# Last pair of the second FFN by tokens, and norm sums over squares added beforehand, in a hybrid encoder layer

## The chip, the cores and the metric

The kernel runs on one core of a Trainium2 chip. Its time is the device time of one launch in microseconds (us), the median of several runs; what a change is worth is judged against the same kernel's runs before it. Engines are named as in the profile: PE (TensorE, matmuls), PEld (its weight loads), DVE (VectorE), ACT (ScalarE), POOL (GpSimd), SP (the engine that issues most DMAs).

## The reference

1088 tokens (1024 of a prompt, 64 of a sample) of width 1024 pass one layer. All is float32.

```python
def _rmsnorm(x, g):
    xf = x.astype(jnp.float32)
    y = xf * lax.rsqrt(jnp.mean(xf * xf, axis=-1, keepdims=True) + EPS)
    return (y * g.astype(jnp.float32)).astype(x.dtype)

def _swiglu_half(x, g, w_gate, w_up, w_down):
    h = _rmsnorm(x, g)
    return 0.5 * ((jax.nn.silu(h @ w_gate) * (h @ w_up)) @ w_down)
...
        xp = xp + _swiglu_half(xp, g_ffn1[l], w1_gate[l], w1_up[l], w1_down[l])
        dp, kp, vp, Cp, n_p, mp = _mix_prompt(xp, rows, *mix_w)
        xp = xp + dp
        xp = xp + _swiglu_half(xp, g_ffn2[l], w2_gate[l], w2_up[l], w2_down[l])
        xp = _rmsnorm(xp, g_final[l])
```

The hidden width of an FFN is 2816. The mixer (projection, windowed attention, mLSTM, output projection) begins with its own `_rmsnorm`.

## The kernel before

**Layout.** The residual x stands transposed, features on partitions: `X` and `X2` are [128, 8, 1088], eight blocks of 128 features by 1088 tokens. Every float32 product that counts is made of three matmuls of the type fp32r (`three_pass`, L248 to L250): high part by high part, high by low, low by high. The high part of an operand is a copy in fp32r by ACT, the low part a subtraction by DVE or POOL.

**Tiles.** The mixer and the down projections work on three token tiles `NTILE` of 364, 362 and 362 tokens; the first stages of an FFN and the output projection on four tiles of 272 (`OT`).

**FFN down projection.** Hidden features go in 11 pairs of 128 (`PAIRS`, the last one is `LAST`). For each pair `pe_down` (L1165 on) makes, for each of three token tiles n and eight output blocks m, six matmuls into one of six banks (`DOWN_BANK`: 0, 1, 2, 3, 6, 7); `dve_x` (L1183 on) adds half of the bank to x. So one pair is 24 groups of six matmuls on PE and 24 additions on DVE (L1194). `AB` holds the pair's activations (high and low), `WB` its weights; `down_high` (ACT) and `down_low`/`down_a_low` (DVE/POOL) prepare them one pair ahead.

**End of the kernel.** After the last pair PE transposes x back to tokens (L2479): nine blocks b of 128 tokens (the last has 64), two halves of 512 features each, into the eight banks in turn. ACT squares and sums each half (L1850), DVE adds the two sums (L2185), ACT takes the root (L1852), DVE the reciprocal (L2187) and multiplies each half by it and by the gain `GF` into `YO` (L2193). SP sends the block out (L1401, L1403). POOL loads `GF` (L1600) after the last matmul of the last pair, because `GF` lies in the memory of that pair's weights `WBe`.

**Norm sums.** A norm in the transposed layout needs, per token, the sum of squares over 1024 features, on every partition. ACT squares x in two halves of four blocks (`norm_square` L264, `start_square` L737); PE multiplies each of the eight blocks of squares with a matrix of ones (`ONES`), in plain float32, into one bank (`norm_sum` L283, `start_sum` L743). Then ACT takes the root (L268, L751), DVE the reciprocal (L288, L755) and the scaled x (L296, L771), ACT the high part (L274, L782), DVE the low part (L303, L786). In the mixer's norm the three sums stand in PE's order inside the last pair of the first FFN: the sum of tile 0 after group m=4 of tile 1, that of tile 1 after group m=5 of tile 2, that of tile 2 after the first projection chain (c=0). The projection chains `M1` (L250 and neighbours, operands HH, HL, WGH, WGL) run tile by tile, four chains c to a tile at first; before chains 0, 4 and 8 PE waits (`norm_wait`) for both halves of the low part of that tile. After chain c, `head_sums(c-1)` (L2217) sums squares per head, and waits for the root of the head sum before it. In the norm of the second FFN the sums of tiles 0 to 2 stand after output chains 37, 41 and 45, that of tile 3 after the first gate chain.

**Order.** Each engine's program is written out by hand; engines meet at counting semaphores. An engine waits in its own order, so everything behind a waiting instruction waits too. `st.sq`, `st.ss`, `st.rs`, `st.rc` count squares, sums, roots and reciprocals; `s_.xadd` counts the additions to x, `fin.y` the halves of `YO` written, `x_tr` the transposed halves. In the mixer's norm ACT's order is: squares of tile 0, root 0, both squares of tile 1, high parts of tile 0, first squares of tile 2, root 1, second squares of tile 2; then, after it has read chain c=0, high parts of tile 1 and root 2; after c=2, high parts of tile 2.

## Time and profile before

| | |
|---|---|
| median of 3 runs | 2059.22 us (2057.47 to 2061.34) |
| the profiled execution's own time | 2060.87 us |
| its span | 2059.0 us |
| mean granted clock of PE | 0.993 |
| PE busy | 2022.5 us |
| DVE, POOL, ACT busy | 1165.6, 711.6, 691.8 us |
| FFN 1 / mixer begins / FFN 2 norm / last pair of FFN 2 | to about 777 us / 777 us / 1249 us / 2009 us |

The profile is of one execution; times inside it count from its span's start. A matmul's listed duration overlaps the next one's, so what a matmul costs PE is the distance between starts, not the duration. A plain float32 matmul with `ONES` leaves two records in the profile; the counts there (x16 for eight) follow from that.

### The profile page before, as it was taken

To read this page: it belongs to the slowest core of one execution; us is meant where nothing else is said; L and a number is where in the kernel's file an instruction comes from. 1 tells how busy PE (TensorE), PEld (TensorE's weight loads), DVE (VectorE), ACT (ScalarE), POOL (GpSimd) and SP (SyncE) were. 2 spreads that over 40 slices of the span, in tenths; PEclk is the share of its full clock that TensorE was granted. 3 is DMA by queue.
4 is the path that set the end of the run, shared out by engine and by line. 5 is a ranking of instruction groups with operands and counts; after the bars stand their busy time and mean duration, and the time that the engine had idled before them with its cause. 6 is when DMAs were issued, how large, how long until landed. Compare 5 with 4: busy or idle time off the path is not lost.

```text
span 2059.0 us, 38383 instructions
## 1 busy us (share of the span) xinstructions
PE 2022.5 (98%) x14285; PEld 1978.0 (96%) x14285; DVE 1165.6 (57%) x2016; ACT 691.8 (34%) x1371; POOL 711.6 (35%) x732
## 2 busy tenths in 40 slices
PE   7999999999999999999999999999999999999996
PEld 7999999999999999989998999999999999999996
DVE  6755444454666666754445654664454544666665
ACT  6333333333111133733335542433333333311112
POOL 2265655554211110131222430046555555411110
PEclk8999999999999999999999999999999999999999
DMA  8122221215422120342331733212112122632202
GB/s 256 43 84 74 87 68 62 88 68 210 156 91 84 42 74 4 99 121 88 99 101 59 209 85 107 74 64 95 62 62 94 62 94 84 235 102 102 91 0 98
DMA packets 151956, 194.62 MB, mean 95 GB/s; under 512 B 11448, under 2 KB 117464, under 8 KB 151872
## 3 DMA queue, kind: packets, MB, share of 16 engines
q1 hardware_dynamic: 144176, 173.85, 25.8%
q0 software_dynamic: 7696, 19.63, 3.0%
q8 instruction: 55, 0.90, 0.2%
q14 instruction: 29, 0.24, 0.0%
HBM read 142.43 MB, written 50.96 MB: 94 GB/s over the span
## 4 chain that ended last, share of the span: by engine, by line
PE 91%; issue 3%; DVE 2%; ACT 2%; DMA 1%; POOL 0%; SPq 0%; DVEq 0%; ACTq 0%; POOLq 0%
PE bank L248 28%; PE bank L250 28%; PE bank L249 28%; PE bank L2275 1%; PE bank L2294 1%; PE bank L2285 1%; PE bank L743 1%; PE bank L283 1%; DVE YO L2193 1%; DMA XIN<-in_x_prompt 1%; DVE RSC L1892 0%; PE bank L2383 0%; PE bank L2375 0%; PE bank L2385 0%; PE bank L2344 0%
## 5 line engine op out<-in xcount | busy, mean ns | idle before, releaser
L1194 DVE SCALAR_TENSOR_TENSOR X<-bank,X 128x362 f32<-128x362 f32 (+1 forms) x528 | 275.1, 533 | 191.0 <-PE bank L250 191.0
L248 PE MATMUL bank<-HH,WGH 128*128 128x362 f32 (+2 forms) x808 | 264.1, 327 | 0.0
L249 PE MATMUL bank<-HL,WGH 128*128 128x362 f32 (+2 forms) x808 | 255.2, 316 | 0.0
L250 PE MATMUL bank<-HH,WGL 128*128 128x362 f32 (+2 forms) x808 | 255.1, 316 | 0.0
L248 PE MATMUL bank<-FC,WR 128*128 128x272 f32 x768 | 223.3, 291 | 2.2 <-ACT X L693 2.0
L250 PE MATMUL bank<-FC,WR 128*128 128x272 f32 x768 | 222.7, 290 | 0.0
L249 PE MATMUL bank<-FC,WR 128*128 128x272 f32 x768 | 221.9, 289 | 0.0
L589 DVE TENSOR_TENSOR PV<-bank,PV 128x272 f32<-128x272 f32 x280 | 122.5, 439 | 148.0 <-PE bank L250 107.9
L656 POOL TENSOR_TENSOR SA<-SA,PV 128x272 f32<-128x272 f32 x160 | 136.5, 874 | 112.8 <-DVE PV L589 109.7
L248 PEld LDWEIGHTS bank<-HH,WGH 128*128 128x128 f32 x808 | 152.8, 189 | 14.7 <-issue 13.0
L469 DVE TENSOR_TENSOR WR<-RAWU,WR 128x512 fp32r<-128x512 f32 x100 | 86.4, 864 | 131.6 <-ACT WR L464 131.6
L248 PE MATMUL bank<-ABe,WBe 128*128 128x362 f32 (+1 forms) x480 | 158.0, 329 | 0.0
L248 PE MATMUL bank<-ABo,WBo 128*128 128x362 f32 (+1 forms) x480 | 157.6, 328 | 0.0
L250 PE MATMUL bank<-ABo,WBo 128*128 128x362 f32 (+1 forms) x480 | 157.1, 327 | 0.0
L250 PE MATMUL bank<-ABe,WBe 128*128 128x362 f32 (+1 forms) x480 | 157.0, 327 | 0.0
L249 PE MATMUL bank<-ABo,WBo 128*128 128x362 f32 (+1 forms) x480 | 157.0, 327 | 0.0
L249 PE MATMUL bank<-ABe,WBe 128*128 128x362 f32 (+1 forms) x480 | 156.9, 327 | 0.0
L249 PEld LDWEIGHTS bank<-HL,WGH 128*128 128x128 f32 x808 | 152.7, 189 | 1.6
L250 PEld LDWEIGHTS bank<-HH,WGL 128*128 128x128 f32 x808 | 152.6, 189 | 0.0
L248 PEld LDWEIGHTS bank<-FC,WR 128*128 128x128 f32 x768 | 145.2, 189 | 3.1 <-issue 2.2
L249 PEld LDWEIGHTS bank<-FC,WR 128*128 128x128 f32 x768 | 145.6, 190 | 0.0
L250 PEld LDWEIGHTS bank<-FC,WR 128*128 128x128 f32 x768 | 145.5, 189 | 0.0
(350 smaller groups left out, 5564.1 us busy)
## 6 DMA issues: line engine op xcount, KB each, us to landing
asp<-SA SPq DMA_DIRECT2D x44, 544.0 KB, 3.1
AR<-asp SPq DMA_DIRECT2D x22, 1088.0 KB, 5.0
RAWG<-in_w_gate SPq DMA_DIRECT2D x22, 1024.0 KB, 5.9
RAWU<-in_w_up SPq DMA_DIRECT2D x22, 1024.0 KB, 5.2
RAWDe<-in_w_down SPq DMA_DIRECT2D x12, 1024.0 KB, 4.9
RAW<-in_w_in SPq DMA_DIRECT2D x22, 512.0 KB, 3.6
RAWDo<-in_w_down SPq DMA_DIRECT2D x10, 1024.0 KB, 5.1
xsp<-X SPq DMA_DIRECT2D x8, 1088.0 KB, 6.1
```

Source lines behind the costliest of these rows:

```text
L248: nc.tensor.matmul(bank[:, 0:w], w_hi, rhs_hi, start=first, stop=False)
L249: nc.tensor.matmul(bank[:, 0:w], w_hi, rhs_lo, start=False, stop=False)
L250: return nc.tensor.matmul(bank[:, 0:w], w_lo, rhs_hi, start=False, stop=last)
L283: mm = nc.tensor.matmul(BANK[NORM_BANK[n]][:, 0:w], ONES[:, :], SQH[:, k, t0:t0 + w], start=(k == 0), stop=(k == KT - 1))
L469: nc.vector.tensor_tensor(WR[:, o, 1], weight(o, q0, mat), WR[:, o, 0].bitcast(F32), ALU.subtract).then_inc(s_.lo, 1)
L589: nc.vector.tensor_tensor(out, bank, add, ALU.add).then_inc(s_.ev, 1)
L656: nc.gpsimd.tensor_tensor(gated(j, slot), gated(j, slot), PV[j][:, tile], ALU.mult).then_inc(s_.mul, 1)
L743: mm = nc.tensor.matmul(BANK[4 + n][:, 0:HT], ONES[:, :], SQT[:, kh, k], start=(kh == 0 and k == 0), stop=(kh == 1 and k == 3))
L1194: nc.vector.scalar_tensor_tensor(out=x, in0=BANK[DOWN_BANK[i % 6]][:, 0:w], scalar=0.5, in1=x, op0=ALU.mult, op1=ALU.add).then_inc(s_.xadd, 1)
L2193: nc.vector.scalar_tensor_tensor(out=YO[0:L, b % 4, c], in0=BANK[(2 * b + half) % 8][0:L, :], scalar=f[:, 3:4], in1=GF[0:L, c], op0=ALU.mu ...
L2275: mm = nc.tensor.matmul(BANK[2 + i // 2][:, (i % 2) * 256:(i % 2) * 256 + 256], QB[rows, par, 2 * g_ + hl // 2, :], KW[rows, par, 0 if g_ ...
L2285: tr = nc.tensor.transpose(BANK[4 + w][:, i * P:(i + 1) * P], SP[:, i, w * P:(w + 1) * P], IDENT[:, :])
```

## The change

1. **The last pair of FFN 2 by tokens.** `pe_down` and `dve_x` of that pair and the transposes behind it are gone. In their place `pe_token_block` takes each block b of tokens and each half of 512 features: four transposes of x put x into the bank, by tokens, and six fp32r matmuls (activations stationary, 512 weight columns moving) add the pair's product on top, in the same bank. The half of the FFN's factor 0.5 goes into the weights' high and low parts. Banks are `TOKEN_BANK`: 4 and 5, 0 and 1, 2 and 3, 6 and 7.
2. **The end follows block by block.** ACT and DVE read the same bank as before, now each block as soon as PE has left it. `GF` lies in the memory of the first pair's weights, and POOL loads it after the second pair. The last block goes out in two DMAs of half its width.
3. **Norm sums.** POOL adds the four blocks of squares of a half to two and then to one (in place), and PE multiplies two blocks with `ONES` where it multiplied eight. Each sum now waits for POOL (`st.add`), not ACT.
4. **Places.** Sum of tile 1 in the mixer's norm: after group m=7 of tile 2 (was m=5). Sum of tile 2: after chain c=2 (was c=0). Sum of tile 3 in FFN 2's norm: after the second gate chain (was the first). Chains 0, 4 and 8 wait for the first half of the low part at their start and for the second at k=4.

```diff
-        GF = place("GF", [P, D], F32, rD)
+        GF = place("GF", [P, D], F32, rWG)
...
-            for k in range(KT):
-                if k % 4 == 0:
-                    pe.wait_ge(st.sq, 9 + 2 * n + k // 4 + 1)
-                mm = nc.tensor.matmul(BANK[NORM_BANK[n]][:, 0:w], ONES[:, :], SQH[:, k, t0:t0 + w], start=(k == 0), stop=(k == KT - 1))
+            for h in range(2):
+                pe.wait_ge(st.add, 4 * n + 2 * h + 2)
+                mm = nc.tensor.matmul(BANK[NORM_BANK[n]][:, 0:w], ONES[:, :], SQH[:, 4 * h, t0:t0 + w], start=(h == 0), stop=(h == 1))
             mm.then_inc(st.ss, 1)
+
+        def norm_add(pool, n, h):
+            t0, w = NTILE[n]
+            k = 4 * h
+            pool.wait_ge(st.sq, 9 + 2 * n + h + 1)
+            nc.gpsimd.tensor_tensor(SQH[:, k:k + 2, t0:t0 + w], SQH[:, k:k + 2, t0:t0 + w], SQH[:, k + 2:k + 4, t0:t0 + w], ALU.add).then_inc(st.add, 1)
+            pool.wait_ge(st.add, 4 * n + 2 * h + 1)
+            nc.gpsimd.tensor_tensor(SQH[:, k, t0:t0 + w], SQH[:, k, t0:t0 + w], SQH[:, k + 1, t0:t0 + w], ALU.add).then_inc(st.add, 1)
...
+        def start_add(pool, n, kh):
+            done = 12 + 4 * n + 2 * kh
+            pool.wait_ge(st.sq, 15 + 2 * n + kh + 1)
+            nc.gpsimd.tensor_tensor(SQT[:, kh, 0:2], SQT[:, kh, 0:2], SQT[:, kh, 2:4], ALU.add).then_inc(st.add, 1)
+            pool.wait_ge(st.add, done + 1)
+            nc.gpsimd.tensor_tensor(SQT[:, kh, 0], SQT[:, kh, 0], SQT[:, kh, 1], ALU.add).then_inc(st.add, 1)
...
-                start_chain(pe, f, 0, 0, 0)
-                start_sum(pe, 3)
-                for i in range(1, 4):
+                for i in range(4):
                     start_chain(pe, f, 0, 0, i)
+                    if i == 1:
+                        start_sum(pe, 3)
...
+        TOKEN_BANK = (4, 0, 2, 6)
...
+        def pe_token_block(pe, b):
+
+            L, t0 = (P if b < NB else DEC), b * P
+            done = 264 + LAST * 24
+            if b == 0:
+                pe.wait_ge(s_.alo, LAST * 2 + (22 + 2))
+                pe.wait_ge(s_.dlo, LAST * 2 + (22 + 2))
+            if b < 4:
+                pe.wait_ge(s_.xadd, done - 24 + (8, 20, 22, 24)[b])
+            else:
+                pe.wait_ge(fin.y, 2 * (b - 3))
+            for half in range(2):
+                bank, c = token_bank(b, half), slice(512 * half, 512 * half + 512)
+                for k in range(4):
+                    nc.tensor.matmul(bank[0:L, k * P:(k + 1) * P], X[:, 4 * half + k, t0:t0 + L], IDENT[:, :], is_transpose=True, start=k == 0, stop=False)
+                for d in range(2):
+                    a_hi, a_lo = (AB[2][:, i, d, t0:t0 + L] for i in range(2))
+                    w_hi, w_lo = (WB[2][:, i, d, c] for i in range(2))
+                    nc.tensor.matmul(bank[0:L, :], a_hi, w_hi, start=False, stop=False)
+                    nc.tensor.matmul(bank[0:L, :], a_hi, w_lo, start=False, stop=False)
+                    mm = nc.tensor.matmul(bank[0:L, :], a_lo, w_hi, start=False, stop=d == 1)
+                mm.then_inc(x_tr, 1)
...
-            pool.wait_ge(s_.dmm, 2 * 264)
+            pool.wait_ge(s_.dmm, 264 + 48)
...
-            pe_down(pe, 0, LAST, 0, 2, between=lambda: norm_sum(pe, norm, 1), at=5)
+            pe_down(pe, 0, LAST, 0, 2, between=lambda: norm_sum(pe, norm, 1), at=KT - 1)
```

Where the instructions stand. First PE's order at the second mixer sum, before; ABe and WBe are the last pair's operands.

```order
1889 L250 MATMUL bank3<-ABe_83,WBe_86 128x362
1890 L283 MATMUL bank5<-SQH_96,ONES_144 128x362 x8
1891 L248 MATMUL bank6<-ABe_83,WBe_86 128x362
1892 L249 MATMUL bank6<-ABe_83,WBe_86 128x362
1893 L250 MATMUL bank6<-ABe_83,WBe_86 128x362
```

And the same sum on PE in the changed kernel (HH, HL, WGH and WGL are the first projection chain's operands).

```order
1901 L250 MATMUL bank7<-ABe_83,WBe_86 128x362
1902 L282 MATMUL bank5<-SQH_96,ONES_144 128x362 x2
1903 L248 MATMUL bank0<-HH_51,WGH_54 128x364
1904 L249 MATMUL bank0<-HL_52,WGH_54 128x364
1905 L250 MATMUL bank0<-HH_51,WGL_55 128x364
```

The sum has two matmuls for eight and has moved behind the last two groups of the last pair, to the mixer's first chain.

POOL's order between the first FFN and the mixer's first store, before.

```order
134 L1159 TENSOR_TENSOR ABe_83<-AR00_88,ABe_83 128x1088 x2
135 L1455 DMA out_7<-in_cache_k 16x512
136 L1456 DMA out_8<-in_cache_v 16x512
137 L1458 MEMSET RAW4_58 128x1024
138 L1476 DMA zqk<-ZST_97 128x364
```

And in the changed kernel (its last four rows stand once more, for the third tile, ahead of the store).

```order
137 L1504 MEMSET RAW4_58 128x1024
138 L289 TENSOR_TENSOR SQH_96<-SQH_96 128x2x364
139 L291 TENSOR_TENSOR SQH_96<-SQH_96 128x364
140 L289 TENSOR_TENSOR SQH_96<-SQH_96 128x2x364
141 L291 TENSOR_TENSOR SQH_96<-SQH_96 128x364
142 L289 TENSOR_TENSOR SQH_96<-SQH_96 128x2x362
143 L291 TENSOR_TENSOR SQH_96<-SQH_96 128x362
144 L289 TENSOR_TENSOR SQH_96<-SQH_96 128x2x362
145 L291 TENSOR_TENSOR SQH_96<-SQH_96 128x362
```

Twelve additions have come between the memset and the store, four for each tile. Eight pairs of the form 128x544 and 128x272 stand likewise ahead of POOL's first weight sum of FFN 2.

Last, PE's order at the end of the kernel, before.

```order
6188 L248 MATMUL bank7<-ABe_83,WBe_86 128x362
6189 L249 MATMUL bank7<-ABe_83,WBe_86 128x362
6190 L250 MATMUL bank7<-ABe_83,WBe_86 128x362
6191 L2479 MATMUL bank0<-IDENT_143,X_49 128x128 x4
6192 L2479 MATMUL bank1<-IDENT_143,X_49 128x128 x4
```

And the first half of the first token block in the changed kernel.

```order
6047 L1197 MATMUL bank4<-IDENT_143,X_49 128x128 x4
6048 L1201 MATMUL bank4<-WBe_86,ABe_83 128x512
6049 L1202 MATMUL bank4<-WBe_86,ABe_83 128x512
6050 L1203 MATMUL bank4<-WBe_86,ABe_83 128x512
6051 L1201 MATMUL bank4<-WBe_86,ABe_83 128x512
6052 L1202 MATMUL bank4<-WBe_86,ABe_83 128x512
6053 L1203 MATMUL bank4<-WBe_86,ABe_83 128x512
6054 L1197 MATMUL bank5<-IDENT_143,X_49 128x128 x4
```

The transposes no longer stand behind all matmuls of the pair; four of them open each of 18 groups, followed by six matmuls of 512 columns.

## Rows read from the trace of the kernel before

**Rows 1.** The page: PE's busy time and the chain that ended last.
```profile
PE 2022.5 (98%) x14285; PEld 1978.0 (96%) x14285; DVE 1165.6 (57%) x2016; ACT 691.8 (34%) x1371; POOL 711.6 (35%) x732
PE 91%; issue 3%; DVE 2%; ACT 2%; DMA 1%; POOL 0%; SPq 0%; DVEq 0%; ACTq 0%; POOLq 0%
```
**Rows 2.** Timeline (start, duration, engine, line, operation), PE, first mixer sum.
```profile
755.95 5.05 PE L283 MATMUL bank<-SQH,ONES 128*128 128x364 f32 x16
...
761.01 0.32 PE L249 MATMUL bank<-ABe,WBe 128*128 128x362 f32 x1
```
**Rows 3.** Timeline, PE, first sum of FFN 2's norm.
```profile
1254.16 3.83 PE L743 MATMUL bank<-SQT,ONES 128*128 128x272 f32 x16
...
1257.95 0.29 PE L249 MATMUL bank<-HL,WGH 128*128 128x272 f32 x1
```
**Rows 4.** POOL: one line's view (min/median/max ns), and one group by form (mean).
```profile
L656 POOL TENSOR_TENSOR SA<-SA,PV x160: 762/773/1678, 110.7 to 1773.7; 128x272 f32<-128x272 f32 x160
...
L1159 POOL TENSOR_TENSOR ABe<-AR,ABe 128x1088 fp32r<-128x1088 f32 x20 | 50.4, 2543 | 176.6 <-ACT ABe L1144 176.6
```
**Rows 5.** Timeline, ACT and DVE, the mixer's norm: squares to low parts.
```profile
751.79 1.42 ACT L264 ACTIVATE SQH<-X 128x1456 f32<-128x1456 f32 x1 [2.58 <-DVE X L1194]
753.69 1.22 DVE L1267 TENSOR_TENSOR WGL<-RAW,WGH 128x1024 fp32r<-128x1024 f32 x1
761.64 2.43 DVE L288 RECIPROCAL SQH<-SQH 128x364 f32<-128x364 f32 x1 [4.28 <-ACT SQH L268]
771.10 1.66 DVE L303 TENSOR_TENSOR HL<-SQa,HH 128x1456 fp32r<-128x1456 f32 x1
773.56 1.66 DVE L303 TENSOR_TENSOR HL<-SQb,HH 128x1456 fp32r<-128x1456 f32 x1
795.56 1.41 ACT L274 ACTIVATE HH<-SQb 128x1448 fp32r<-128x1448 f32 x1
798.92 0.57 ACT L1632 ACTIVATE RSC<-bank,EPSC 128x364 f32<-128x364 f32 x1
```
**Rows 6.** Timeline, POOL and DVE side by side in FFN 2.
```profile
1509.96 1.30 POOL L452 TENSOR_TENSOR RAWG<-RAWG,SS 128x512 f32<-128x512 f32 x1 [1.72 <-DVE WR L469]
1510.33 1.47 DVE L469 TENSOR_TENSOR WR<-SS,WR 128x512 fp32r<-128x512 f32 x1
```
**Rows 7.** Timeline, ACT, last squares of FFN 2's norm.
```profile
1296.03 2.10 ACT L737 ACTIVATE SQT<-X 128x1088 f32<-128x1088 f32 x2
```
**Rows 8.** Timeline, PE: last pair's first and last matmul, and transposes.
```profile
2009.08 0.33 PE L248 MATMUL bank<-ABe,WBe 128*128 128x364 f32 x1
2032.67 0.32 PE L250 MATMUL bank<-ABe,WBe 128*128 128x362 f32 x1
2033.62 3.71 PE L2479 MATMUL bank<-IDENT,X 128*128 128x128 f32 x32 [0.63 <-DVE X L1194]
```
**Rows 9.** Timeline, PE: 16 transposes between two fp32r chains, FFN 1.
```profile
26.79 1.91 PE L687 MATMUL bank<-IDENT,XIN 128*128 128x128 f32 x16
...
28.67 0.29 PE L249 MATMUL bank<-FC,WR 128*128 128x272 f32 x1
```
**Rows 10.** Timeline, DVE, ACT and SP: the end, first block, then last block.
```profile
2035.60 1.28 ACT L1852 ACT_TABLE_LOAD   x1
2037.28 0.16 DVE L2185 TENSOR_TENSOR FS<-FS 128x1 f32<-128x1 f32 x1 [3.71 <-DMA GF<-in_g_final]
2039.33 0.15 DVE L2185 TENSOR_TENSOR FS<-FS 128x1 f32<-128x1 f32 x1
...
2052.49 0.58 ACT L1850 ACTIVATE JUNK<-bank 64x512 f32<-64x512 f32 x1
2053.57 0.14 DVE L2185 TENSOR_TENSOR FS<-FS 64x1 f32<-64x1 f32 x1
2055.69 0.55 SPq L1403 DMA_DIRECT2D out<-YO  x1
```
**Rows 11.** Windows: stretch, length, busy of PE, PEld, DVE, ACT, POOL; clock, DMA, GB/s.
```profile
26.00:30.00 4.00, 4.00 (x36) 4.00 (x35) 4.00 (x10) 2.08 (x3) 0.00 (x0) 1.00 1.03 400
2040.00:2050.00 10.00, 6.31 (x38) 4.55 (x35) 8.03 (x19) 7.07 (x26) 0.00 (x0) 0.83 0.66 264
```

More of the change, by code:

```diff
@@ L740, in start_sum @@
             for kh in range(2):
-                pe.wait_ge(st.sq, 15 + 2 * n + kh + 1)
-                for k in range(4):
-                    mm = nc.tensor.matmul(BANK[4 + n][:, 0:HT], ONES[:, :], SQT[:, kh, k], start=(kh == 0 and k == 0), stop=(kh == 1 and k == 3))
+                pe.wait_ge(st.add, 12 + 4 * n + 2 * kh + 2)
+                mm = nc.tensor.matmul(BANK[4 + n][:, 0:HT], ONES[:, :], SQT[:, kh, 0], start=(kh == 0), stop=(kh == 1))
             mm.then_inc(st.ss, 1)
+        def start_add(pool, n, kh):
[4 more added lines that the diff above has]
+            nc.gpsimd.tensor_tensor(SQT[:, kh, 0], SQT[:, kh, 0], SQT[:, kh, 1], ALU.add).then_inc(st.add, 1)
         def scale_row(f, n):
@@ L1126, in up_pe, with by_token @@
                     pe_stage(pe, f, p, i // 2, i % 2)
+        def by_token(f, p):
+            return f == 1 and isinstance(p, int) and p == LAST
         def a_raw(f, odd, start):
@@ L1146, in down_high @@
                 act.wait_ge(s_.d_in1 if odd else s_.d_in0, loads)
-                nc.scalar.activation(WB[which][:, 0, i], RAWD[odd][:, i], ACT.Copy).then_inc(s_.dhi, 1)
+                nc.scalar.activation(WB[which][:, 0, i], RAWD[odd][:, i], ACT.Copy, scale=0.5 if by_token(f, p) else 1.0).then_inc(s_.dhi, 1)
         def down_low(dve, f, p, odd, i, start=False):
@@ L1271, in loads_until, with unit_chain @@
             return (j - 4) // 4 + 1 if j % 4 == 0 else (j - j % 4) // 4 + 1 + (j % 4 == 1)
-        def unit_chain(pe, n, slot, bank, tiles=NTILE, k0=0, k1=KT):
+        def unit_chain(pe, n, slot, bank, tiles=NTILE, k0=0, k1=KT, second=None):
             t0, w = tiles[n]
             for k in range(k0, k1):
+                if k == 4 and second is not None:
+                    pe.wait_ge(second, n + 1)
                 mm = three_pass(bank, w, WGH[:, slot, k], WGL[:, slot, k], HH[:, k, t0:t0 + w], HL[:, k, t0:t0 + w], k == k0, k == k1 - 1)
@@ L1395, in _ @@
             ffn_sp(sp, 1, a["w2_gate"][0], a["w2_up"][0], a["w2_down"][0])
[L1398 removed]
+            for b in range(NB):
                 sp.wait_ge(fin.y, 2 * b + 2)
[L1400 to L1403 removed]
+                sp.dma_start(o[0][0, b * P:(b + 1) * P, :], YO[:, b % 4, :]).then_inc(fin_out[b % 4], 16)
+            for half in range(2):
+                c = slice(512 * half, 512 * half + 512)
+                sp.wait_ge(fin.y, 2 * NB + half + 1)
+                sp.dma_start(o[1][0, :, c], YO[0:DEC, NB % 4, c]).then_inc(fin_out[NB % 4], 16)
             for i in range(4):
[L1405 removed]
+                sp.wait_ge(fin_out[i], 16 * ((NB - i) // 4 + 1 + (i == NB % 4)))
         @block.gpsimd
@@ L1458, in _ @@
             nc.gpsimd.memset(RAW4[:, 1, :, :], 0.0).then_inc(z.padded, 1)
+            for n in range(3):
+                for h in range(2):
+                    norm_add(pool, n, h)
             flat = lambda ap: ap.rearrange("p h d -> p (h d)")
@@ L1593, in _ @@
             pool.dma_start(o[10][0, 0].rearrange("h d -> d h"), CNS[:, :, LD]).then_inc(m_.cout, 16)
+            for n in range(4):
+                for kh in range(2):
+                    start_add(pool, n, kh)
             pool.wait_ge(m_.cout, 96)
@@ L2175, in _ @@
             down_dve(dve, 1)
-            for n in range(3):
-                dve_x(dve, 1, LAST, n)
             dve.wait_ge(const_in, 16 * 12)
@@ L2242, in _ @@
             for c, (j, n) in enumerate(M1):
-                if c < 12 and c % 4 == 0:
-                    norm_wait(pe, norm, n)
+                opens = c < 12 and c % 4 == 0
+                if opens:
+                    pe.wait_ge(norm.lo0, n + 1)
                 pe.wait_ge(z.lo, j)
@@ L2252, in _ @@
                     pe.wait_ge(z.zg, NORMED.index(c - 4) + 1)
-                unit_chain(pe, n, j % 4, BANK[c % 4])
+                unit_chain(pe, n, j % 4, BANK[c % 4], second=norm.lo1 if opens else None)
                 if c == C1 - 1:
@@ L2257, in _ @@
                     head_sums(c - 1)
-                if c == 0:
+                if c == 2:
                     norm_sum(pe, norm, 2)
@@ L2467, in _ @@
             down_pe(pe, 1)
-            for n in range(3):
-                pe_down(pe, 1, LAST, 0, n)
-            pe.wait_ge(s_.xadd, 2 * 264)
             for b in range(NB + 1):
-                L = P if b < NB else DEC
-                if b >= 4:
-                    pe.wait_ge(fin.y, 2 * (b - 3))
-                for half in range(2):
-                    for k in range(4):
-                        tr = nc.tensor.transpose(BANK[(2 * b + half) % 8][0:L, k * P:(k + 1) * P], X[:, 4 * half + k, b * P:b * P + L], IDENT[:, :])
-                    tr.then_inc(x_tr, 1)
+                pe_token_block(pe, b)
 _INS = ["x_prompt", "x_sample", "cache_k", "cache_v", "state_C", "state_n", "state_m", "g_ffn1", "w1_gate", "w1_up", "w1_down",
```

23 lines of the change are left out of this document (10 added, 13 removed).

## The prediction

> **What bounds the kernel now.** I read the page first: PE is busy for 98% of the span, and 91% of the chain that ended last is PE's [rows 1]. So an instruction taken from PE shortens the kernel by what it costs there, unless PE then waits for what is late next. I read the two norms in the timeline next, since the sums stand in PE's order: PE has no idle time around them, and the squares are ready when it comes [rows 2, 3, 5]. Last I read the end. PE's last fp32r matmul starts at 2032.67 [rows 8], the span ends at 2059.0: 26 us in which PE only transposes and the rest waits, first for `GF`, to 2037.28, then nine times for one round of DVE and ACT, 2.05 us each (2037.28 to 2039.33), then for the last DMA, from 2055.69 to the span's end [rows 10]. This stretch is bound by DVE with ACT.
>
> **Sums off PE.** Eight matmuls with `ONES` at 364 columns take from 755.95 to 761.01, less one normal distance of 0.165 us: 4.9 us, 0.61 each [rows 2]. Six fewer: 3.65 us; three sums: 10.9 us. (The distance 0.165 is (2032.67 - 2009.08) / 143, the 144 matmuls of the last pair [rows 8].) In FFN 2's norm eight at 272 columns take 1254.16 to 1257.95, less about 0.13: 3.66 us, 0.455 each [rows 3]. Six fewer, four sums: 10.9 us. Together 21.8 us if nobody else becomes late.
>
> **What POOL's additions cost.** 272 elements take POOL 0.773 us, 1088 take 2.54 [rows 4], so by a line 364 take 0.97, 544 take 1.36 and 728 take 1.76. A half of squares costs POOL 2.7 us in the mixer, 2.1 us in FFN 2. POOL is otherwise idle at both places. But POOL and a DVE instruction that reads two operands from SBUF do not run side by side: DVE's L469, 128x512, takes 1.47 us where POOL's addition is under way at its start (1509.96 to 1511.26), and it ends some 0.5 us after that [rows 6]. The scale (L296), the low parts (L303) and the weights' low parts (L1267) are such instructions. The Trainium skill's GPSIMD Engine Reference, section Key points, says that the two engines share their SBUF interfaces and collide when a DVE instruction has two SBUF inputs; the trace agrees. Were additions and DVE's work free to run side by side, against that rule, the sum below would be about 3 us larger.
>
> **The mixer's norm, worked through.** (a) Tile 0. The second squares end at 753.21 [rows 5]; POOL would be done 2.7 us later, at 756.0. DVE's L1267 (1.22 us, wanted at 753.69 [rows 5]) falls in between and I give it to DVE first: 757.2. PE wants the sum at 755.95. Stall 1.3 us. Everything behind the sum on PE, the last pair's last eleven groups, waits with it. (b) Chain 0. The root now comes 2.0 us earlier than before (sum over at 758.6, not 760.57), and so does DVE's chain behind it: reciprocal (2.43), scale, low parts, which ended at 772.76 and 775.22 [rows 5]. But POOL's additions for tiles 1 and 2 fall into this chain's scale and second low part and take back a microsecond or more each. Low parts ready at about 771.5 and 775. PE, with two sums shorter (7.3 us) and 1.3 us late, comes to chain 0 at 770.5. It waits about 1.3 us at the start and 1.5 at k=4: 2.9 us. (c) The third sum has moved behind c=2, at about 785. ACT's root 2 stands ahead of its high parts of tile 2, and these ahead of its reads of chain 3. Root at 787, reciprocal and two scales on DVE (2.4 and 2 times 2.1) to 793.7, second high part to 795.2, then squares, copy and root for `head_sums` to 796.7; PE comes to the second `head_sums`, behind c=4, at 795.1. Stall 1.6 us. Before, this chain had slack: the high part started at 795.56 and the root at 798.92 with PE at 802 [rows 5]. Chains 4 and 8 find their low parts ready (783 and 796 at the latest). Sum for the mixer: 10.9 - 1.3 - 2.9 - 1.6 = 5.1. Bounds: 8 where DVE loses nothing to POOL, 2.5 where each meeting costs a full addition (1.8 us).
>
> **FFN 2's norm.** The squares of tiles 0 and 1 come several us before PE does. Those of tile 2 end about 1277.7 once PE is 5.4 us earlier; POOL, sharing with two low parts on DVE, is done at 1281.2, PE comes at 1280.5: 0.7 us. Those of tile 3 ended at 1298.13 [rows 7], now at 1290.6 because PE's output chains pace them; POOL needs two times 2.1 us and meets DVE's scale and low parts: 1294.2 to 1296. PE comes, behind its second gate chain, at 1294.5. I take 1.0 us. Sum: 10.9 - 1.7 = 9.2; bounds 10.5 and 6. POOL's weight sums for the next pair are in the same queue behind these additions, but wait for a transfer that comes later (they began at 1304.0 in the trace of before), so that costs nothing.
>
> **The last pair and the end.** Removed from PE: the 144 matmuls, 2009.08 to 2032.83, and 72 transposes. Added: 72 transposes and 108 matmuls of 512 columns. 32 transposes take 3.41 to 3.5 us [rows 8]: 0.107 each. A change from fp32r to transposes and back costs little: 16 transposes and the return take 28.67 - 26.79 - 0.13 = 1.75 us, of which 1.71 is the transposes [rows 9]; I take 0.05 for each of two in a block. No 512-column fp32r matmul is in the trace. The nearest is 0.165 us at 362 to 364 columns: in proportion 512 take 0.233; with only the 149 added columns at the full clock of 2.4 GHz, 0.165 + 0.062 = 0.227. I take 0.230. A block: 8 x 0.107 + 12 x 0.230 + 0.1 = 3.72 us, nine: 33.4 us. The last block has 64 tokens, but its moving columns are the same. PE starts at 2009.08 as before (block 0 needs the operands and eight additions of the pair before, which are long past; banks 4 and 5 are free) and ends at 2042.5, drained by 2042.7. ACT and DVE need 2.05 us for a block, under 3.72, so they keep up; block b+4 waits for a `YO` that was written about 10 us before. `GF`'s 3.7 us wait and the 1.28 us table load [rows 10] go beside PE's work. Behind the last matmul: squares 0.67, then from DVE's addition to SP's issue 2055.69 - 2053.57 = 2.12, then the DMA to the span's end 3.3 (2059.0 - 2055.69) [rows 10]; it now carries half, I give it the full 3.3. End at 2042.7 + 0.67 + 0.05 + 2.12 + 3.3 = 2048.8. Gain 10.2 us. Bounds: 13 (0.22 a matmul, 2.5 for the DMA) and 6 (0.24 a matmul and 0.15 a change). The low part of the last weights becomes a scalar_tensor_tensor; it runs some 15 us before it is needed and costs nothing.
>
> **Sum.** 5.1 + 9.2 + 10.2 = 24.5 us. The profiled span 2059.0 becomes 2034.5, its own time 2060.87 becomes 2036.4. That execution lies 1.65 above the median 2059.22, so the median becomes 2034.7; I say 2035.
>
> **Rivals.** (1) *No losses to POOL:* PE finds every sum ready and no chain late: 21.8 + 10.2 = 32.0, 2027. For: PE is the bound everywhere. Against: the arithmetic of (a), where POOL cannot be done in time. (2) *The sums give nothing:* DVE's norm chains become the bound and hand back all of what PE saves; only the end gains: 2049. For: chain 0 starts right behind the low parts already. Against: of FFN 2's norm only the last two sums meet a late partner. (3) *The clock falls in the token blocks:* in 2040 to 2050, where PE ran only transposes with gaps, its granted clock was 0.83 [rows 11]. If it went to 1.2 GHz, half, for all nine blocks, they would take 66.8 us instead of 33.4, and the kernel 2035 + 33.4 = 2068: slower. It turns slower from 24.5 / 3.72, between six and seven blocks at the half clock. Against: 26 to 30 us has transposes among fp32r chains at a clock of 1.00 [rows 11], and a block is three quarters fp32r. (4) *The matmuls on top of transposed x are slower:* at 0.46 us each instead of 0.23 they cost 24.8 us more, and the change is worth nothing. Nothing in the trace speaks for it.
>
> **How the numbers follow.** The forecast, with stalls anywhere within the bounds: 0.70, from 2059.2 - 31.5 = 2028 to 2059.2 - 14.5 = 2045. Rival 1: 0.12. Rival 2: 0.10. Rival 3: 0.04. Rival 4 and what I have not seen: 0.04. All bounds at once at their bad end are unlikely, so the range stops at 2043 and takes in rival 1's edge: 2026 to 2043. About 4 us, 0.2%, is what a measurement can tell from no change. Faster: 0.93; same: 0.03; slower: 0.04.
>
> **What would show it.** In the timeline of after: two-matmul sums of 1.2 and 0.9 us; a PE wait of some 1 us on POOL at the first mixer sum, 2 to 3 us at chain 0 for DVE's low parts, 1 to 2 us at the second `head_sums` on ACT, and one of about 1 us on POOL at the last sum of FFN 2's norm. At the end: token blocks 3.7 us apart, clock 1.00, and 6 to 6.5 us from PE's last matmul to the span's end. The prediction is wrong if the blocks lie over 4.2 us apart, if PE waits for `fin.y`, or if the waits at the norms sum to under 3 or over 15 us.

## The result, and the profile after

The changed kernel takes 2033.19 us (median of 4 runs, 2031.86 to 2033.58), the kernel before beside it 2059.31 (4 runs, 2057.47 to 2061.34). The ratio is 0.9872, 95% interval 0.9855 to 0.9889: 26 us faster. The forecast was 2035 in a range of 2026 to 2043. The profiled execution's own time is 2033.58, its span 2032.0.

The page of after first, PE's busy time and the chain that ended last, which answer to [rows 1]:

```profile
PE 1999.2 (98%) x14165; PEld 1954.1 (96%) x14165; DVE 1165.3 (57%) x1992; ACT 692.9 (34%) x1371; POOL 751.2 (37%) x760
PE 94%; DVE 2%; ACT 1%; DMA 1%; POOL 1%; issue 1%; SPq 0%; DVEq 0%; ACTq 0%; POOLq 0%
```

PE has 23 us less to do and is still the bound; POOL has 40 us more, nearly all of it additions of squares. DVE's total is the same although its last 24 additions to x are gone (12.7 us by the sum of their line): instructions that now meet POOL have grown by about as much, 32 scales of the second FFN's norm alone from 13.9 to 20.6 us. Then PE's waits in after, one group by line, releaser, total, times and longest:

```profile
PE bank L2265 <- ACT RSC L1684: 5.3, 4, 1.6
PE bank L248 <- DVE HL L310: 2.9, 2, 1.5
...
PE bank L744 <- POOL SQT L752: 0.9, 1, 0.9
```

The second and third groups are new, and the first had three waits before where it has four now. The timeline of PE in after shows where they stand in the mixer's norm (the last bracket is the idle time ahead of the instruction, and who ended it):

```profile
754.04 0.77 PE L282 MATMUL bank<-SQH,ONES 128*128 128x364 f32 x2
755.09 0.88 PE L282 MATMUL bank<-SQH,ONES 128*128 128x364 f32 x2 [0.28 <-POOL SQH L291]
...
769.62 0.43 PE L248 MATMUL bank<-HH,WGH 128*128 128x364 f32 x1 [1.49 <-DVE HL L310]
773.27 0.43 PE L248 MATMUL bank<-HH,WGH 128*128 128x364 f32 x1 [1.39 <-DVE HL L310]
...
794.85 0.85 PE L2265 MATMUL bank<-SQC,BD 128*128 128x364 f32 x2 [1.54 <-ACT RSC L1684]
```

The first sum (it answers to [rows 2]) loses 0.28 us to POOL, chain 0 loses 1.49 at its start and 1.39 at k=4 to DVE's low parts, the second `head_sums` 1.54 to ACT. In the second FFN's norm the same view has three sums that matter (they answer to [rows 3]):

```profile
1247.68 1.08 PE L744 MATMUL bank<-SQT,ONES 128*128 128x272 f32 x4
...
1275.14 0.72 PE L744 MATMUL bank<-SQT,ONES 128*128 128x272 f32 x2 [0.86 <-POOL SQT L752]
...
1287.81 1.45 PE L744 MATMUL bank<-SQT,ONES 128*128 128x272 f32 x4
```

The third sum waits 0.86 us for POOL. The fourth shows no wait, but its records span 1.45 us where the first sum's span 1.08: up to 0.4 us went there.

The end, PE in after: the transposes that open a half, in blocks 7 and 8, and the last matmul.

```profile
2018.96 0.60 PE L1197 MATMUL bank<-IDENT,X 128*128 128x128 f32 x4
2020.80 0.60 PE L1197 MATMUL bank<-IDENT,X 128*128 128x128 f32 x4
2022.64 0.60 PE L1197 MATMUL bank<-IDENT,X 128*64 128x128 f32 x4
...
2026.04 0.40 PE L1203 MATMUL bank<-WBe,ABe 128*64 128x512 f32 x1
```

Blocks lie 2022.64 - 2018.96 = 3.68 us apart. The windows of after over this stretch (length, busy time and count of PE, PEld, DVE, ACT, POOL, then the granted clock, DMA share and GB/s; they answer to [rows 11]):

```profile
1992.00:2010.00 18.00, 18.00 (x101) 15.16 (x101) 7.04 (x18) 7.86 (x21) 0.00 (x0) 1.00 0.22 89
2010.00:2026.00 16.00, 16.00 (x89) 12.75 (x88) 7.95 (x18) 7.37 (x22) 0.00 (x0) 1.00 0.33 132
```

PE has no gap and its clock is full, 2.4 GHz. Behind PE, the timeline of DVE, ACT and SP (they answer to [rows 10]):

```profile
1997.88 1.28 ACT L1904 ACT_TABLE_LOAD   x1
...
2027.19 0.15 DVE L2233 TENSOR_TENSOR FS<-FS 64x1 f32<-64x1 f32 x1 [1.50 <-ACT JUNK L1902]
...
2027.89 1.40 DVE L2241 SCALAR_TENSOR_TENSOR YO<-bank,FS,GF 64x512 f32<-64x512 f32 x2
2028.67 1.19 SPq L1449 DMA_DIRECT2D out<-YO  x2
```

The table load lies beside PE's first blocks. From PE's last matmul (2026.04 + 0.40) to the span's end are 5.56 us.

**Where the 27.0 us of the spans came from.** Six events stand in every kernel's trace, so distances between them can be subtracted: A, ACT's first squares of the mixer's norm; B, PE's second `head_sums`; C, PE's first sum of the second FFN's norm; D, PE's first matmul behind it that reads `FXb`, an operand of the gate and up chains; E, the start of the last pair; F, the span's end, which is given to 0.1 us only.

| kernel | start to A | A to B | B to C | C to D | D to E | E to F |
|---|---|---|---|---|---|---|
| before | 747.79 | 54.00 | 452.37 | 96.15 | 658.77 | 49.92 |
| after | 745.87 | 48.98 | 452.83 | 86.85 | 658.78 | 38.69 |
| gain | 1.92 | 5.02 | -0.46 | 9.30 | 0.0 | 11.23 |

A to B is the mixer's norm, C to D the second FFN's, E to F the end. Nothing is changed ahead of A. From B to C only the split wait of chain 8 is, and from D to E only the load of `GF` and the making of the last weights; PE waits for none of them. Kernels with the same instructions there differ by as much or more (start to A 745.19 to 747.82 in the table of all kernels, B to C 452.83 to 457.28 in three profiles of the changed kernel alone), so these differences are not counted as the change's.

### The profile page after: what moved, and what is told of

Its sections match the earlier page's. It is cut to its first block, busy times and chain, and to the rows that moved or that the text cites. A ratio compares the mean times of both kernels' runs of the same rounds, so it can differ in the third digit from the quotient of the medians.

```text
span 2032.0 us, 38145 instructions
## 1 busy us (share of the span) xinstructions
PE 1999.2 (98%) x14165; PEld 1954.1 (96%) x14165; DVE 1165.3 (57%) x1992; ACT 692.9 (34%) x1371; POOL 751.2 (37%) x760
## 4 chain that ended last, share of the span: by engine, by line
PE 94%; DVE 2%; ACT 1%; DMA 1%; POOL 1%; issue 1%; SPq 0%; DVEq 0%; ACTq 0%; POOLq 0%
PE bank L248 29%; PE bank L250 29%; PE bank L249 29%; PE bank L2324 1%; PE bank L2343 1%; PE bank L2334 1%; DMA XIN<-in_x_prompt 1%; PE bank L2265 0%; PE bank L2432 0%; PE bank L1203 0%; PE bank L1201 0%; PE bank L1202 0%; PE bank L2424 0%; PE bank L1197 0%; PE bank L2434 0%
## 5 line engine op out<-in xcount | busy, mean ns | idle before, releaser
L1237 DVE SCALAR_TENSOR_TENSOR X<-bank,X 128x362 f32<-128x362 f32 (+1 forms) x504 | 262.4, 533 | 178.9 <-PE bank L250 178.9
L517 ACT ACTIVATE SA<-SA 128x272 f32<-128x272 f32 x160 | 67.0, 429 | 227.7 <-DVE SA L591 118.6
L248 PE MATMUL bank<-ABe,WBe 128*128 128x362 f32 (+1 forms) x432 | 142.0, 329 | 0.0
L250 PE MATMUL bank<-ABe,WBe 128*128 128x362 f32 (+1 forms) x432 | 141.7, 328 | 0.0
```

What stands on the lines that cost most here:

```text
L248: nc.tensor.matmul(bank[:, 0:w], w_hi, rhs_hi, start=first, stop=False)
L250: return nc.tensor.matmul(bank[:, 0:w], w_lo, rhs_hi, start=False, stop=last)
L517: nc.scalar.activation(tile, tile, ACT.Silu).then_inc(s_.silu, 1)
L1237: nc.vector.scalar_tensor_tensor(out=x, in0=BANK[DOWN_BANK[i % 6]][:, 0:w], scalar=0.5, in1=x, op0=ALU.mult, op1=ALU.add).then_inc(s_.xadd, 1)
```

## The experiments

All are measured against the kernel before, in runs beside it. Some kernels are built from the changed kernel by undoing parts.

**1. The changed kernel again**, without an edit, as a partner for the parts.

> The changed kernel once more, as the measure for the three parts beside it. All theories: 2033 us or 26 us under the kernel before, within 2 us.

Measured: 2037.66 us beside 2062.02, ratio 0.9878 [0.9861, 0.9894]. A to B is 48.96, C to D 86.85, E to F 38.68: all three within 0.02 us of the first profile. B to C is 457.28, over 4 us more than in the other two profiles of this kernel (452.83 and 453.23). Part of that is the clock. In this trace the granted clock (seventh figure) is 0.50 to 0.65 from 1206 to 1214 us, where the first profile has 1.00 at the same place:

```profile
1208.00:1210.00 2.00, 2.00 (x9) 1.86 (x9) 1.75 (x7) 0.00 (x0) 0.00 (x0) 0.50 0.00 0
```

Two-microsecond windows like this one put its cost at 3.4 us at most: that is what the clock was short of full in them. So the stages that the change touches repeat closely (A to B and E to F to hundredths; C to D is 86.64 in a third profile), and the medians scatter at least in part by what happens elsewhere.

**2. The last pair by tokens alone.** Cut, against the changed kernel:

```diff
             for h in range(2):
-                pe.wait_ge(st.add, 4 * n + 2 * h + 2)
-                mm = nc.tensor.matmul(..., SQH[:, 4 * h, t0:t0 + w], ...)
+            for k in range(KT):
+                if k % 4 == 0:
+                    pe.wait_ge(st.sq, 9 + 2 * n + k // 4 + 1)
+                mm = nc.tensor.matmul(..., SQH[:, k, t0:t0 + w], ...)
...
-            for n in range(3):
-                for h in range(2):
-                    norm_add(pool, n, h)
```

> The last pair by tokens alone, all norm sums as before. My account (the end is worth 11.2 us by the two traces, 10.2 by the prediction's sum): 10 to 11.5 us under the kernel before, 2048 to 2049.5 us. Rival (the end's gain was helped by the sums, or the sums are worth all 22 us and the end little): under 7 us.

Measured: 2050.63, ratio 0.9941 [0.9927, 0.9954], 11.4 us under before. E to F is 38.75, 11.17 less than before; A to B 54.01 and C to D 96.15, as before.

**3. The mixer's sums alone**, and **4. the second FFN's sums alone.** In each the other norm and the end stand as before; in the third, for instance:

```diff
-            return f == 1 and isinstance(p, int) and p == LAST
+            return False
...
-            for n in range(4):
-                for kh in range(2):
-                    start_add(pool, n, kh)
```

> Only the three sums of the mixer's norm, with POOL's additions and the new places; FFN 2's norm and the end as before. My account: PE saves 10.9 us and waits 5 to 6 us more, net 4.5 to 5.5 us under the kernel before; in the trace, waits of 0.3 to 1.3 us for POOL at the first sum, 2.9 at chain 0, 1.5 at the second head sum. Rival (no losses to POOL and DVE): 10.9 us under. Rival (DVE's chain gives everything back): 0 to 1 us.

> Only the four sums of FFN 2's norm, with POOL's additions and the new place of the last; mixer's norm and the end as before. My account: 9 to 10 us under the kernel before, PE waiting about 1.3 us for POOL in all. Rival (POOL meets DVE at every sum): under 7 us.

Measured: the mixer's alone 2055.93, ratio 0.9964 [0.9951, 0.9978], 6.1 us under before; the second FFN's alone 2050.31, ratio 0.9943 [0.9928, 0.9957], 11.7 under. By stages: A to B 48.97 in the one (5.03 less) and 54.01 in the other; C to D 96.38 and 86.87 (9.28 less). By medians the three parts add up to 29.2, more than the whole gives beside them (24.4). By stages they add up to 11.17 + 5.03 + 9.28 = 25.5, and the whole is 11.23 + 5.02 + 9.30 = 25.6. So the parts are independent. The last two medians give 1 to 2.5 us more than their stages; the stretches that no part touches vary by more than that, so the surplus is put down to them, which is not shown.

**5. The three sums back at their old places**, with POOL's additions kept.

```diff
-                    if i == 1:
+                    if i == 0:
                         start_sum(pe, 3)
...
-            pe_down(pe, 0, LAST, 0, 2, between=lambda: norm_sum(pe, norm, 1), at=KT - 1)
+            pe_down(pe, 0, LAST, 0, 2, between=lambda: norm_sum(pe, norm, 1), at=5)
...
-                if c == 2:
+                if c == 0:
                     norm_sum(pe, norm, 2)
```

> The changed kernel with the three moved sums back at their old places (mixer's tile 1 after m=5, tile 2 after chain 0, FFN 2's tile 3 after the first gate chain), all additions still on POOL. Theory that the moves are what covers POOL's time: PE waits for POOL about 1.5 us more at the mixer's third sum and 3 to 3.5 us at FFN 2's last, the wait at the second head sum goes, net 3 to 5 us slower than the changed kernel. Rival (places do not matter, POOL is early enough): within 1 us of it, with POOL waits as before.

Measured: 2041.71 beside 2060.78, ratio 0.9903 [0.9886, 0.992]. PE's timeline of this kernel has three waits for POOL that the changed kernel doesn't have:

```profile
780.35 0.88 PE L282 MATMUL bank<-SQH,ONES 128*128 128x362 f32 x2 [2.45 <-POOL SQH L291]
...
1288.20 0.72 PE L744 MATMUL bank<-SQT,ONES 128*128 128x272 f32 x2 [1.13 <-POOL SQT L752]
1290.61 1.28 PE L744 MATMUL bank<-SQT,ONES 128*128 128x272 f32 x2 [1.68 <-POOL SQT L752]
```

A to B is 49.98 and C to D 91.34, 1.0 us more in the mixer and 4.5 more in the second FFN, 5.5 together, where 3 to 5 were expected. But not all of the 4.5 is waiting. Behind the last of these waits the granted clock was at half:

```profile
1290.00:1292.00 2.00, 1.39 (x4) 1.16 (x5) 2.00 (x3) 0.08 (x1) 0.55 (x1) 0.64 0.91 312
1292.00:1294.00 2.00, 2.00 (x11) 2.00 (x11) 2.00 (x3) 1.97 (x3) 1.56 (x1) 0.51 0.02 3
```

The matmuls of 272 columns stand 0.23 us apart there instead of 0.125, and from the sum's last matmul (1290.61) to the eleventh start behind it (1293.95) PE needs 3.3 us for what takes 1.8 in the changed kernel. So about 1.5 us of the 4.5 is the clock and 3.0 the waits with their restarts: the places are worth some 4 us by themselves, as expected. Whether the fall belongs to this kernel or to this one execution isn't known. In the mixer the wait for POOL (2.45) is partly paid for by the wait at the second `head_sums`, which is gone.

**6. ACT's high parts later.** The wait at the second `head_sums` was put down to ACT's order: its high parts of tile 2 stand ahead of its reads of chain 3. The timeline of ACT in the changed kernel:

```profile
790.00 1.43 ACT L274 ACTIVATE HH<-SQa 128x1448 fp32r<-128x1448 f32 x1 [3.46 <-DVE SQa L303]
792.02 1.42 ACT L274 ACTIVATE HH<-SQb 128x1448 fp32r<-128x1448 f32 x1 [0.60 <-DVE SQb L303]
793.34 0.45 ACT L1699 ACTIVATE SQC<-bank 128x364 f32<-128x364 f32 x1
793.69 0.56 ACT L1702 ACTIVATE ZST<-bank,GQ 128x364 f32<-128x364 f32 x1
794.14 0.57 ACT L1684 ACTIVATE RSC<-bank,EPSC 128x364 f32<-128x364 f32 x1
```

```diff
-                if c == 2:
+                if c == 3:
```

> The changed kernel; ACT makes the high parts of tile 2 after its reads of chain 3, not after those of chain 2. Theory (the new head-sum wait comes from ACT's order: high parts queued ahead of chain 3's squares and the root): the first of the four waits L2265 for RSC, 1.5 us, is gone, 1.5 us faster. Rival (the wait is that of a late DVE or of PE's own earlier arrival): it stays or moves to chain 8.

Measured: 2033.13, ratio 0.9865 [0.9849, 0.9882], 27.7 under before. PE's waits in this kernel, the same group as above:

```profile
PE bank L2265 <- ACT RSC L1684: 3.7, 3, 1.6
```

The fourth wait is gone, and A to B falls from 48.98 to 47.29: 1.69 us, the wait and its restart. The cause is shown.

**7. POOL's additions for tile 2 behind the low part.** The wait at k=4 was put down to POOL and DVE not running side by side. The timelines of DVE and POOL in the changed kernel:

```profile
760.22 3.96 DVE L303 SCALAR_TENSOR_TENSOR SQa<-X,GC,SQH 128x364 f32<-128x364 f32 x4
...
764.99 2.11 DVE L303 SCALAR_TENSOR_TENSOR SQb<-X,GC,SQH 128x364 f32<-128x364 f32 x4
...
767.91 1.66 DVE L310 TENSOR_TENSOR HL<-SQa,HH 128x1456 fp32r<-128x1456 f32 x1
...
770.37 2.85 DVE L310 TENSOR_TENSOR HL<-SQb,HH 128x1456 fp32r<-128x1456 f32 x1
```

```profile
759.79 0.97 POOL L291 TENSOR_TENSOR SQH<-SQH 128x362 f32<-128x362 f32 x1
761.83 1.96 POOL L289 TENSOR_TENSOR SQH<-SQH 128x724 f32<-128x724 f32 x1 [1.07 <-ACT SQH L264]
...
769.93 1.76 POOL L289 TENSOR_TENSOR SQH<-SQH 128x724 f32<-128x724 f32 x1 [4.92 <-ACT SQH L264]
771.77 2.28 POOL L291 TENSOR_TENSOR SQH<-SQH 128x362 f32<-128x362 f32 x1
```

A scale of the same form takes 2.11 us alone and 3.96 beside POOL, the same low part 1.66 and 2.85; POOL's short addition takes 0.97 alone and 2.28 beside DVE. The starts tell who pays. The second low part starts at 770.37, while POOL's long addition runs until 769.93 + 1.76 = 771.69, and it is that addition's remaining 1.3 us by which the low part is late, 1.2 us; the addition itself keeps its 1.76. POOL's short addition then starts at 771.77, while the low part runs until 773.22, and it is the short one that is stretched, by 1.3 us. So whoever starts second waits for the other to finish. The edit:

```diff
                 for h in range(2):
+                    if n == 2 and h == 0:
+                        pool.wait_ge(norm.lo1, 1)
                     norm_add(pool, n, h)
```

> The changed kernel; POOL's additions for the mixer's tile 2 start only when DVE has written the second low part of tile 0. Theory (POOL's addition and DVE's subtraction with two SBUF operands exclude each other): that low part takes 1.66 us again, not 2.85, and PE's wait at k=4 of chain 0 falls from 1.4 to 0.2 us; 1.2 us faster. Rival (the low part is late for another reason, and POOL merely slows itself): wait unchanged.

Measured: 2033.33, ratio 0.9869 [0.9853, 0.9886]. DVE's second low part in this kernel's timeline:

```profile
770.54 1.66 DVE L310 TENSOR_TENSOR HL<-SQb,HH 128x1456 fp32r<-128x1456 f32 x1
```

With POOL held back it takes 1.66 us, and PE's wait at k=4 is 0.20 instead of 1.39. A to B is 47.94, 1.04 less: the wait at the second `head_sums` has grown from 1.54 to 1.69. The collision is shown as the cause of the wait at k=4. It moved in part here too: the first scale of tile 1 takes 3.99 us in this kernel instead of 3.53, but PE doesn't come to wait for that tile's low parts.

**8. Both edits, and a third:** POOL's second additions for tile 1 wait for DVE's first scale, to free that scale too.

```diff
+                    if n == 1 and h == 1:
+                        pool.wait_ge(st.ht, 8 + 1)
```

> The two edits before together, and POOL's second additions for tile 1 wait for DVE's first scale of tile 0 (which took 3.96 us, 2.11 alone). Theory: the waits at chain 0 fall from 2.9 to about 1.0 us, the first head-sum wait is gone, in all 3 to 3.5 us faster than the changed kernel, 29 to 30 us under the kernel before. Rival (DVE's chain is paced by PE's additions to x and not by POOL): under 2 us.

Measured: 2033.55, ratio 0.9864 [0.9848, 0.9881]. Half of it came. The first scale fell from 3.96 to 2.46 us, but POOL's addition now met the second scale, which grew from 2.11 to 3.67: the collision had moved. And something else stood in chain 0, in the windows of this kernel:

```profile
770.00:772.00 2.00, 1.02 (x5) 1.03 (x6) 2.00 (x4) 1.65 (x2) 0.00 (x0) 0.94 0.00 0
772.00:774.00 2.00, 2.00 (x8) 2.00 (x8) 2.00 (x3) 0.00 (x0) 0.53 (x1) 0.50 0.00 0
774.00:776.00 2.00, 2.00 (x11) 2.00 (x10) 2.00 (x2) 1.41 (x1) 1.92 (x2) 0.70 0.00 0
```

and in PE's timeline:

```profile
770.98 0.43 PE L248 MATMUL bank<-HH,WGH 128*128 128x364 f32 x1 [1.84 <-DVE HL L310]
...
772.32 0.50 PE L248 MATMUL bank<-HH,WGH 128*128 128x364 f32 x1
772.62 0.51 PE L249 MATMUL bank<-HL,WGH 128*128 128x364 f32 x1
```

The granted clock (seventh figure) was 0.50, that is 1.2 GHz, in 772 to 774, a microsecond behind a wait of 1.84 us, and ten matmuls stand 0.30 us apart instead of 0.165. A to B is 47.22, hardly less than the 47.29 of experiment 6.

**9. The same kernel once more**, to see whether that fall belongs to it.

> The kernel with all three edits once more. In its first profile PE waited 1.84 us for the low part at the start of chain 0, and some 1 us later the granted clock was 0.50 in 772 to 774 us: ten matmuls of chain 0 stood 0.30 us apart instead of 0.165. Theory (what PE does around that wait brings the fall): the fall comes again at the same place, with ten or eleven matmuls 0.30 apart, and from ACT's first squares to PE's second head sum there are 47.2 us again. Rival (a chance event of that execution): no matmul of chain 0 is over 0.2 us from the next except at its start, and the stretch takes 46.1 us or less, as in the kernel with two edits (46.07).

Measured (2 runs): 2031.9 beside 2064.23, ratio 0.9846 [0.9817, 0.9874]. The rival held in substance. The same stretch in the windows of this run, and chain 0 in its timeline of PE:

```profile
770.00:772.00 2.00, 1.80 (x11) 1.50 (x10) 2.00 (x3) 0.00 (x0) 0.51 (x1) 1.00 0.00 0
772.00:774.00 2.00, 2.00 (x14) 2.00 (x13) 2.00 (x2) 1.57 (x2) 1.92 (x2) 1.00 0.00 0
```

```profile
769.00 0.43 PE L248 MATMUL bank<-HH,WGH 128*128 128x364 f32 x1 [1.68 <-DVE HL L310]
```

The wait was 1.68 here, the clock stayed full, and A to B is 46.15 (46.1 or less was said), 1.07 less than in experiment 8; at k=4 PE waited 0.20. So the fall comes in some executions and not in others, and costs about 1.1 us where it comes. What decides it stays open.

**10. The changed kernel as partner, and the two edits that had worked** (late high parts, POOL's wait for tile 2), without the third.

> The changed kernel itself, unchanged, as the partner of the two kernels beside it: 26 us under before, within 2; PE waits 1.5 us for ACT's root at the second head sum and 2.9 us for DVE's low parts at chain 0.

> Two edits to the changed kernel: ACT's high parts of tile 2 stand behind its reads of chain 3, and POOL's additions for tile 2 wait for the second low part of tile 0. Theory (a wait taken from PE's path comes off the time): PE's wait at the second head sum (1.5 us) and the one at k=4 of chain 0 (1.4 us) go, and nothing else becomes late: 2.7 us less than the changed kernel beside it, by medians 1 to 4.5 less. Rival (the time of the mixer's first chains is set elsewhere, by DVE or a DMA that comes later, so that waits only change their place): the same time within 1 us, with new PE waits of 2 to 3 us behind chain 4.

Measured beside before at 2061.28: the changed kernel 2037.48 (2034.7 to 2042.99), ratio 0.9892 [0.9875, 0.9909]; with the two edits 2034.29 (2032.05 to 2035.44), ratio 0.9869 [0.9852, 0.9887]. PE's timeline with the two edits:

```profile
770.23 0.44 PE L248 MATMUL bank<-HH,WGH 128*128 128x364 f32 x1 [1.48 <-DVE HL L310]
772.70 0.43 PE L248 MATMUL bank<-HH,WGH 128*128 128x364 f32 x1 [0.20 <-DVE HL L310]
...
792.57 0.78 PE L2267 MATMUL bank<-SQC,BD 128*128 128x364 f32 x2
```

A to B is 46.07 against 48.96: 2.89 us, where 2.7 was expected; the two single edits gave 1.69 and 1.04, 2.73 together. The medians differ by 3.2 and agree, but their intervals overlap; the stage distance carries the verdict that the two edits help. This is the version to keep: the third edit adds nothing to it (46.15 without the fall).

**11. The last block in one DMA** of full width instead of two of half of it.

```diff
-            for half in range(2):
-                c = slice(512 * half, 512 * half + 512)
-                sp.wait_ge(fin.y, 2 * NB + half + 1)
-                sp.dma_start(o[1][0, :, c], YO[0:DEC, NB % 4, c])...
+            sp.wait_ge(fin.y, 2 * NB + 2)
+            sp.dma_start(o[1][0, :, :], YO[0:DEC, NB % 4, :])...
```

> The changed kernel with the last block of 64 tokens written by one DMA of full width, behind both halves, instead of two of half the width. Theory (the last DMA is paid from its issue to the end, and the second half's issue was bound by DVE's last multiplication in either form): SP's issue comes at the same time as that of the second half before, about 20.6 us... that is 3.2 us before the end, and the landing takes 0.3 to 0.9 us longer for 256 KB than for 128: from PE's last matmul to the end 5.9 to 6.5 us, was 5.6. Rival (each of the two issues costs SP 0.6 us in a row, which is on the path): the single DMA ends 0.2 to 0.5 us earlier. By the medians neither can be seen; by the trace, from the last matmul to the span's end.

(The "20.6 us" in that text is a slip; what was meant follows it.) Measured: 2037.74, ratio 0.9887 [0.9869, 0.9906]. PE's last matmul in this trace, and SP's issue:

```profile
2030.40 0.40 PE L1203 MATMUL bank<-WBe,ABe 128*64 128x512 f32 x1
```

```profile
2033.68 0.55 SPq L1447 DMA_DIRECT2D out<-YO  x1
```

The span ends at 2037.0: 6.20 us behind PE's last matmul, was 5.56; E to F is 39.33, was 38.69. Splitting the last DMA is worth 0.64 us, and the rival (two issues in a row cost more than they bring) falls.

**The stages of all kernels**, in us:

| kernel | start to A | A to B | B to C | C to D | D to E | E to F |
|---|---|---|---|---|---|---|
| changed, 3 profiles | 745.87 to 746.44 | 48.96 to 48.98 | 452.83 to 457.28 | 86.64 to 86.85 | 658.78 to 661.18 | 38.68 to 38.69 |
| last pair alone | 746.63 | 54.01 | 453.40 | 96.15 | 660.16 | 38.75 |
| mixer alone | 747.78 | 48.97 | 452.97 | 96.38 | 658.61 | 49.79 |
| second FFN alone | 745.21 | 54.01 | 451.59 | 86.87 | 659.20 | 49.92 |
| old places | 747.64 | 49.98 | 452.21 | 91.34 | 660.28 | 38.75 |
| high parts later | 747.82 | 47.29 | 452.53 | 86.85 | 660.35 | 38.66 |
| POOL waits | 746.05 | 47.94 | 452.39 | 86.85 | 660.06 | 38.71 |
| two edits | 746.50 | 46.07 | 453.12 | 86.64 | 660.62 | 38.75 |
| three edits (first run) | 747.17 | 47.22 | 452.23 | 86.84 | 660.41 | 38.73 |
| three edits (second run) | 745.19 | 46.15 | 453.93 | 86.86 | 660.08 | 38.69 |
| last DMA whole | 746.70 | 48.97 | 454.32 | 86.86 | 660.82 | 39.33 |

## Why the prediction was right

**The whole.** 24.5 us were forecast from three terms; the same three stages give 5.02 + 9.30 + 11.23 = 25.55 in the traces. What is left to the 27.0 of the spans, 1.92 - 0.46, stands in stretches that hold the same instructions. It made the gain look a little larger in the first measurement; by medians it was 26.1 us there and 24.4 and 23.8 when the same kernel was run again.

**The mixer's norm: 5.1 forecast, 5.02 measured.** Its terms:
- The first sum, for POOL: 1.3 forecast, 0.28 seen. This step failed in two places. POOL ended at 753.21 + 1.82 = 755.03, that is 9.16 us behind A; the forecast had 757.2, 9.4 behind. And the forecast let PE stand from the start of the sum, while only the second of its two matmuls needs POOL's last addition: the first, 0.61 us, runs meanwhile.
- Chain 0: 2.9 forecast, 1.49 + 1.39 measured. Right, and the low parts came when the forecast said, 23.7 and 27.4 us behind A for 23.7 and 27.2. Experiment 7 shows the mechanism for the wait at k=4: POOL beside DVE. For the wait at the start it stays argued: it was 1.47 to 1.84 in every kernel with these sums, and experiment 8 only moved POOL from the first scale to the second.
- The second `head_sums`: 1.6 forecast, 1.54 measured; experiment 6 shows the mechanism, ACT's order.
- The waits sum to 4.7, and 10.9 - 4.7 is 6.2, not 5.0. The missing term is what a stop costs PE beside the wait, which the forecast put at nothing. The distances between starts give it: at k=4 the two matmuls stand 1.71 us apart, 1.55 over the normal distance for a wait of 1.39, and the next one follows after 0.27 instead of 0.165. Read so, the first sum costs 0.55, chain 0 1.75 and 1.65, and the second `head_sums` 1.70. A fifth stop has no wait in its row; a weight load waited there for DVE's addition to x, which stands behind the stretched first scale:

```profile
764.68 0.43 PE L248 MATMUL bank<-ABe,WBe 128*128 128x362 f32 x1
```

It starts 0.30 us behind the one before and costs 0.25 with its restart. Together that is 5.9, and 10.9 - 5.9 = 5.0. So two errors of the forecast, 1.0 us too much at the first sum and 1.2 us left out, cancelled: that the sum is closer than its parts is luck.

**The second FFN's norm: 9.2 forecast, 9.30 measured.** The third sum's wait was 0.86 (0.7 forecast), the fourth's at most 0.4 (1.0 forecast). The fourth term was too large for the same reason as in the mixer: the first matmul of the sum covers half a microsecond of the wait (POOL was done at 1288.47, PE had come at 1287.81). With their restarts the two sums cost 1.1 and 0.4 us, 1.5 together for the 1.7 forecast; another 0.2 us of the stage isn't accounted for. And POOL's weight sums behind the additions cost nothing, as said.

**The end: 10.2 forecast, 11.23 measured.** The blocks are right: 3.68 us for 3.72, no wait for `fin.y`, clock 1.00, the table load and `GF` hidden. PE's share of the end, 1993.31 to 2026.44, is 33.1 for 33.6: half of the 1.0 us. The other half lies behind PE, 5.56 us where the forecast had 6.1 and said 6 to 6.5. There the mis-sized term is the last DMA: 3.3 us were given to it because the whole one had taken that; split in two it takes 2.7 from the second issue (SP's two issues end at 2028.67 + 1.19, one takes 0.55, so the second began at 2029.31, and the span ends at 2032.0), and experiment 11 measures the split at 0.64.

**The rivals.** No losses to POOL: wrong by the 4.7 us of waits, the causes of two of which were then removed (experiments 6 and 7). The sums give nothing: excluded by experiments 3 and 4. The clock at half in the token blocks: the windows say 1.00 there. Slow matmuls on top of transposed x: they stand 0.23 us apart, so no.

**The exclusion.** The forecast counted POOL and DVE as unable to run side by side where DVE reads two operands from SBUF, on a single pair of rows [rows 6]. Experiments 7 and 8 bear it out, with 1.66 against 2.85 us and 2.11 against 3.96 for instructions of the same form. The Trainium skill's GPSIMD Engine Reference, section Key points, says that the two engines share their SBUF interfaces, with contention where a DVE instruction has two SBUF inputs; the traces agree.

## What to carry to other kernels

Work taken from the bounding engine comes off the time one for one, less the new waits and, here, about a quarter of a microsecond for each stop. When an operand comes can be forecast to some tenths of a microsecond if one walks through each engine's queue in its written order; take care which instruction of a group really needs the late operand. When work goes to an idle engine, the price is not its own time but whom it meets: here an addition of 1.76 us on POOL, begun 0.4 us earlier, made a DVE instruction on the path 1.2 us late, and one wait that moves the addition out of the way gave that back. Judge an edit of 1 to 3 us by the distance between two events around it, which repeated within 0.02 us in two stages here and within 0.21 in the third, not by medians, which differed by 4.5 us for the same kernel. Read the granted clock between the two events as well: in experiments 5 and 8 a fall of it stood in the distance and was no part of the edit's waits.
